# A hybrid encoder layer on one core: the first half of branch A's output projection by seven products, gate terms added by DMA, merged rows turned one block sooner

## The reference, cut to what matters

```python
proj = h @ w_in[l]                      # h: (512, 2048) after LayerNorm
...
branches = (oa * silu(ag), ob * silu(bg), oc * silu(cg))    # each (512, 1024)
merged = None
for n in range(3):
    gate = sigmoid(mg[..., n*2048:(n+1)*2048] + b_gate[l, n])
    term = gate * (branches[n] @ w_branch[l, n])            # w_branch: (3, 1024, 2048)
    merged = term if merged is None else merged + term
y = merged @ w_out[l]
h = layer_norm(alpha * h + y, ln_g[l], ln_b[l])
```

## Time and profile before

| | us |
|---|---|
| three timed runs | 1806.41, 1807.3, 1809.01 |
| their median | 1807.3 |
| profiled execution, span (no time of its own is given beside it) | 1805.6 |
| PE, DVE, ACT busy in it | 1791.1, 1368.5, 906.6 |
| stage 3 within it, four halved groups and four plain blocks | 152.4 and 92.4 |

### The profile page before, as it was taken

The page is one execution under the profiler, slowest core; times in us unless marked ns, Lnnn a source line. Parts: engine busy times, 40 slices in busy tenths (PEclk is TensorE's granted clock), DMA queues, the critical chain, the costliest instruction groups (busy, mean ns, idle before and its releaser), DMA issues.

```text
span 1805.6 us, 24177 instructions
## 1 busy us (share of the span) xinstructions
PE 1791.1 (99%) x8365; PEld 1487.6 (82%) x8365; DVE 1368.5 (76%) x2243; ACT 906.6 (50%) x1540; POOL 245.2 (14%) x313
## 2 busy tenths in 40 slices
PE   9999999999999999999999999999999999999997
PEld 7888888888888888888888888888888888888886
DVE  6777774887777877577778878788788787757778
ACT  5663332555465655444445545455555666435543
POOL 1111110100222221001000101101111000002223
PEclk9999999999999999999999999999999999999999
DMA  9576776960865545366566867868696978739989
GB/s 336 180 211 164 194 201 205 260 233 15 227 185 170 176 133 147 104 160 172 119 202 177 257 127 225 216 144 245 129 285 145 310 257 293 262 129 236 238 211 197
DMA packets 250440, 355.49 MB, mean 197 GB/s; under 512 B 14641, under 2 KB 141681, under 8 KB 247025
## 3 DMA queue, kind: packets, MB, share of 16 engines
q1 hardware_dynamic: 178640, 201.61, 35.3%
q0 software_dynamic: 71568, 152.50, 35.1%
q10 hardware_dynamic: 144, 0.26, 0.0%
HBM read 303.30 MB, written 97.11 MB: 222 GB/s over the span
## 4 chain that ended last, share of the span: by engine, by line
PE 97%; DMA 1%; DVE 1%; issue 0%; ACT 0%; POOL 0%; POOLq 0%; DVEq 0%; SPq 0%; ACTq 0%
PE acc L745 10%; PE acc L747 10%; PE acc L746 10%; PE scores L957 6%; PE scores L959 6%; PE scores L961 6%; PE acc L957 3%; PE acc L959 3%; PE acc L961 3%; PE transposed L770 3%; PE attended L959 2%; PE attended L957 2%; PE attended L961 2%; PE scores L1178 2%; PE scores L1180 2%; PE scores L1182 2%
## 5 line engine op out<-in xcount | busy, mean ns | idle before, releaser
L1428 ACT ACTIVATE piece_split<-w 128x512 fp32r<-128x512 f32 x448 | 282.8, 633 | 290.5 <-PE scores L961 104.9
L2069 DVE TENSOR_TENSOR piece_split<-w,piece_split 128x512 fp32r<-128x512 f32 x448 | 309.1, 691 | 104.0 <-ACT piece_split L1428 94.1
L1921 DVE TENSOR_TENSOR w_lo<-raw_weights,w_hi 128x1024 fp32r<-128x1024 f32 x205 | 249.2, 1220 | 140.1 <-ACT w_hi L1323 138.4
L745 PE MATMUL acc<-h_hi,w_lo 128*128 128x512 f32 x800 | 319.2, 399 | 0.0
L747 PE MATMUL acc<-h_hi,w_hi 128*128 128x512 f32 x800 | 312.5, 391 | 0.0
L746 PE MATMUL acc<-h_lo,w_hi 128*128 128x512 f32 x800 | 311.7, 390 | 0.0
L1323 ACT ACTIVATE w_hi<-raw_weights 128x1024 fp32r<-128x1024 f32 x205 | 217.0, 1060 | 130.0 <-PE acc L747 27.3
L747 PEld LDWEIGHTS acc<-h_hi,w_hi 128*128 128x128 f32 x800 | 150.2, 188 | 32.3
L745 PEld LDWEIGHTS acc<-h_hi,w_lo 128*128 128x128 f32 x800 | 150.4, 188 | 29.9 <-issue 1.8
L746 PEld LDWEIGHTS acc<-h_lo,w_hi 128*128 128x128 f32 x800 | 150.6, 188 | 28.6
L957 PE MATMUL scores<-piece_split,h_lo 128*128 128x512 f32 x384 | 149.9, 390 | 0.2 <-DVE piece_split L2069 0.2
(11 more groups left out here) (502 smaller groups left out, 3691.5 us busy)
## 6 DMA issues: line engine op xcount, KB each, us to landing
w<-in_w_in SPq DMA_DIRECT2D x128, 512.0 KB, 9.4
raw_weights<-in_w_in SPq DMA_DIRECT2D x102, 512.0 KB, 4.0
anch_weight_sums_scratch<-in_w_branch POOLq DMA_DIRECT2D x24, 1024.0 KB, 10.2
raw_weights<-in_w_branch SPq DMA_DIRECT2D x40, 512.0 KB, 5.5
raw_weights<-in_w_mem_kv SPq DMA_DIRECT2D x32, 512.0 KB, 5.6
raw_weights<-anch_weight_sums_scratch SPq DMA_DIRECT2D x32, 512.0 KB, 5.8
gate_scratch<-in_b_gate POOLq DMA_DIRECT2D x12, 1024.0 KB, 11.8
gate<-gate_scratch POOLq DMA_DIRECT2D x12, 1024.0 KB, 9.2
```

Of the source, the lines that this page charges most:

```text
L745: pe.matmul(bank_out, wl, hi[:, k, :], start=first, stop=False)
L1428: act.activation(p_split[:, n % RING, 0, :], sources[p][:, k, :], ACT.Copy).then_inc(pc_hi, 1)
L1921: dve.tensor_tensor(w_lo[:, slot, :], raw[:, slot, :], w_hi[:, slot, :].bitcast(F32), ALU.subtract).then_inc(lo_ready, 1)
L2069: dve.tensor_tensor(p_split[:, n % RING, 1, :], sources[p][:, k, :], p_split[:, n % RING, 0, :].bitcast(F32), ALU.subtract).then_inc(pc_lo, 1)
```

## The change

The constants: `HALVED` goes to 5, and two plain blocks (`PLAIN`) stay, nb = 2 and 3. The fifth halved group (s = 4) is branch A's columns 0 to 1023. Its left operands are cut from the same branch A buffer: low and high parts of four pairs of channel rows and of the sums S1 to S4, made by `branch_a_sum`, `branch_a_hi` and `branch_a_lo` in the order of the tables `A_HI` and `A_LO` at fixed steps of the fourth and fifth group. In groups s = 2, 3 and 4 three transfers a group (`add_terms`) add the gate terms to `merged_rows`; only the G4 quarter is still added by DVE. A fourth slot of weight sums, at G7, stands in each gate group. Blocks 0 and 1 are turned in chunks 1 and 2 of the first plain block, block 2 in chunk 1 of the second. The roles of PSUM banks acc and (scores 2, attended) swap behind the groups, and all counts of semaphores follow.

```diff
-CH_PLAIN = CH_M + 56
-CH_OUT = CH_PLAIN + 4 * (D // 512)
+CH_PLAIN = CH_M + 70
+CH_OUT = CH_PLAIN + 4 * (D // 512 - 2)
...
-HALVED = 4
+HALVED = 5
+PLAIN_FROM = 2
+PLAIN = D // 512 - PLAIN_FROM
...
+TERMS = 6
+MERGED_FILLS = {(0, 1): 0, (0, 2): 1, (1, 1): 2}
+A_HI = (("rows", 0), ("sum", 3), ("rows", 2), ("rows", 4), ("sum", 0), ("rows", 6), ("sum", 1), ("sum", 2))
+A_LO = (("sum", 3), ("rows", 0), ("rows", 2), ("sum", 1), ("rows", 4), ("rows", 6), ("sum", 0), ("sum", 2))
...
             def halved_product(s, p, banks, first, stop):
+                if s == HALVED - 1:
+                    pick = branch_a_tiles(p)
+                    hi, lo = pick(bra_hi, as_hi), pick(bra_lo, as_lo)
+                    needed = {G1: ("rows", 2), G5: ("sum", 3), G6: ("sum", 1), G2: ("rows", 6), G7: ("sum", 0),
+                              G3: ("sum", 2), G4: ("rows", 6)}[p]
+                    pe.wait_ge(branch_ready, 2 * PRODUCTS + A_LO.index(needed) + 1)
...
             def fill_merged(nb, j):
-                if j == 0:
-                    pe.wait_ge(m_sum, SUMMED + TT * (nb + 1))
+                if j == 0 and nb < PLAIN_FROM:
+                    pe.wait_ge(terms_added[nb], TERMS_BASE + 16 * (1 + nb) * (HALVED - 2))
+                    pe.wait_ge(m_sum, SUMMED)
+                elif j == 0:
+                    pe.wait_ge(m_sum, SUMMED + TT * (nb - PLAIN_FROM + 1))
...
-                        if m and s == 1:
-                            fill_merged(m - 1, 2 * kk)
-                            fill_merged(m - 1, 2 * kk + 1)
+                        if (m, s) in MERGED_FILLS:
+                            fill_merged(MERGED_FILLS[m, s], 2 * kk)
+                            fill_merged(MERGED_FILLS[m, s], 2 * kk + 1)
...
+            branch_a_hi_at = dict(zip(((3, 1), (3, 3), (3, 5), (3, 8), (3, 10), (3, 11), (3, 12), (4, 5)), A_HI))
...
+            branch_a_sum_at = {(3, 1): (0,), (3, 5): (1,), (3, 7): (2,), (4, 1): (3,), (4, 2): (4,)}
+            branch_a_lo_at = dict(zip(((3, 4), (3, 6), (3, 8), (4, 1), (4, 3), (4, 4), (4, 6), (4, 7)), A_LO))
...
             def halved_gates(s, b, half, src, sign):
-                if s >= 2:
-                    first = {(0, 0): 0, (1, 1): 2, (1, 0): 4}[b, half]
-                    for t in range(2):
-                        row = 2 * half + t
-                        dve.wait_ge(term_made, 6 * (s - 2) + first + t + 1)
-                        dve.tensor_tensor(sums[nb][:, row, :], sums[nb][:, row, :], gate[b][:, row, :], ALU.add)\
-                            .then_inc(m_sum, 1)
...
             def store_group(g):
-                    for n, p in enumerate((G5, G6, G2)):
+                    for n, p in enumerate((G5, G6, G2, G7)):
...
+            def add_terms(s):
+
+                for n, (b, half) in enumerate(((0, 0), (1, 1), (1, 0))):
+                    rows = slice(2 * half, 2 * half + 2)
+                    pool.wait_ge(term_made, TERMS * (s - 2) + 2 * n + 2)
+                    pool.dma_start(sums[2 * (s % 2) + b][:, rows, :], gate[b][:, rows, :], accum_op=ALU.add)\
+                        .then_inc(terms_added[b], 16)
...
-            for m in (*range(1, 2 * HALVED - 2), 2 * HALVED - 1, 2 * HALVED - 2,
-                      *range(2 * HALVED, 2 * HALVED + D // 512)):
+            for m in (1, 2, 3, 4, 5, 7, 6, 9, 8, 10, 11):
...
+                if m in (7, 9, 10):
+                    add_terms((m - 1) // 2 - 1 if m % 2 else HALVED - 1)
                 load_gate(m)
...
-                if m >= 2 * HALVED:
-                    pool.dma_start(out_t[m - 2 * HALVED], ln_b[0].partition_broadcast(P)).then_inc(preset, 16)
+                if m >= 2 * (HALVED - 1):
+                    pool.dma_start(out_t[m - 2 * (HALVED - 1)], ln_b[0].partition_broadcast(P)).then_inc(preset, 16)
```

More of the change, by code:

```diff
@@ L324, in branch_tiles, with branch_a_tiles, branch_a_part @@
         return lambda whole, summed: whole[:, rows, tok]
+    def branch_a_tiles(p):
+        if p in (G5, G6, G7, G3):
+            n = {G5: 3, G6: 1, G7: 0, G3: 2}[p]
+            return lambda whole, summed: summed[:, n, :, :]
+        return branch_tiles(p)
+    def branch_a_part(part):
+        kind, n = part
+        if kind == "sum":
+            return as_hi[:, n, :, :], as_raw[:, n, :, :], as_lo[:, n, :, :]
+        return bra_hi[:, n:n + 2, :], bra_raw[:, n:n + 2, :], bra_lo[:, n:n + 2, :]
     def branch_weights(n, half, right):
@@ L1215, in _ @@
             pe.wait_ge(ev_c12, 2 * ALL + 2)
-            for m in range(D // 512):
+            for m in range(PLAIN):
                 for s in range(4):
@@ L2615, in _ @@
                         halved_lo(1, G2 + j - 1)
-                    if s == 3 and 1 < j < 6:
-                        branch_lo(j - 2)
+                    if (s, j) in branch_a_lo_at:
+                        branch_a_lo(*branch_a_lo_at[s, j])
+                    for n in branch_a_sum_at.get((s, j), ()):
+                        branch_a_sum(n)
             def add_branch(m):
+                nb = PLAIN_FROM + m
                 dve.wait_ge(gate_ready, 2 * HALVED + m + 1)
+                dve.wait_ge(terms_added[m % 2], TERMS_BASE + 16 * (1 + m % 2) * (HALVED - 3))
                 for t in range(TT):
@@ L2631, in add_branch @@
                     dve.wait_ge(m_free, TT * m + t + 1)
[L2632 removed]
+                    dve.tensor_tensor(sums[nb][:, t, :], sums[nb][:, t, :], gate[m % 2][:, t, :], ALU.add)\
                         .then_inc(m_sum, 1)
[L2635 removed]
+            last_m = PLAIN - 1
             steps = Steps(dve, dve_once, OUT_STEPS, base=LN_STEPS + F_STEPS + PRESET_STEPS)
@@ L2672, in double_lo @@
                 dve.tensor_tensor(lo, whole, hi.bitcast(F32), ALU.subtract).then_inc(pc_lo, 1)
-            for m in range(last_m + 1):
+            for m in range(PLAIN):
                 for s in range(4):
```

142 lines of the change are left out of this document (88 added, 54 removed).

## The result

| | us |
|---|---|
| the kernel before, 20 runs | median 1807.21 (1806.16 to 1809.34) |
| the changed kernel, 20 runs | median 1810.14 (1807.58 to 1813.54) |
| ratio | 1.0015, 95% interval 1.0009 to 1.0022 |
| profiled execution of the changed kernel | 1808.13, span 1806.3 |

The change costs 2.7 us by the ratio (2.9 between the medians) instead of gaining 3.0. This is within the 0.2% (3.6 us) that I called no change, but the time is above my whole range (1801.0 to 1808.5). The profiled execution is itself 2.0 us under the median, so what follows explains the profile first and the median only in part.

The account below looks back on a forecast made before the run. PE, busy 99%, was taken to bound the kernel: span 1805.6 - 5.4 (fewer matmuls) + 2.4 (wait) = 1802.6 us. With the 1.7 us offset to the median, the forecast was 1804.3 us, range 1801.0 to 1808.5.

Parts of the forecast that it names:

- 24 matmuls at 0.2268 us, 5.4 us: Fifth halved group: 168 matmuls replace 192 of two plain column blocks, saving 5.4 us on PE.
- Gate terms: Third to fifth groups: nine 512 KB adding transfers, landing in 6.9 to 8.9 us, delay later gate loads at no cost.
- burst: Fifth group: two gate loads and two preset writes, 4 MB issued at once by POOL, slowing weight loads beside them.
- The fifth group's operands: here I expect a wait: At G7, S3's low part comes late behind chunk 9: 9.4 + 11.4 + 3.4 - 21.8 = 2.4 us of PE wait.
- slowed by each other's queue rather than by a full engine: Fifth group: loads in the burst are delayed by sharing between queues; chunk 9's landing taken as 11.4 us.
- equal halves: Fifth group: if queues' turns were equal, a load takes 9.2 us, about twice 4.6, and the wait is 0.2 us.
- Weight sums: cost 0, bounds 0 and 3: End of the first gate group: the new slot's copies finish by 997.3, or 1003.3 if consecutive; cost 0 to 3 us.
- rival 3: Extra weight sums hit the gate groups' weight loads; PE waits up to 3 us; 2 us gives 1806.3; chance 0.07.
- The earlier turning hidden by 1.3 us: Start of the plain part: first turn comes 8.2 us after the last product, its additions end at 6.9; cost 0.
- Offset of 1.7 us from span to median: Whole kernel: the earlier median, 1807.3, lies 1.7 us above the profiled span; carried over to the forecast.

Follow-up runs that it names:

- kernel 14: The changed kernel without its nine adding transfers (terms missing from the output) and with presets moved to gate loads 10 and 11: 1804.41 us, ratio 0.9984.
- kernel 1: The changed kernel without its nine adding transfers, so their gate terms are missing from the output: 1808.07 us, ratio 1.0004.
- experiment 7: The changed kernel with S3's low part made after the split of chunk 8 instead of chunk 9: 1810.58 us, ratio 1.0019.
- experiment 4: The changed kernel with one slot of weight sums moved from the first gate group that has them to the last: 1809.67 us, ratio 1.0013.
- kernel 13: On kernel 9, the low part of rows 6 and 7 made before the split of chunk 7: 1804.89 us, ratio 0.9987.
- kernel 9: The changed kernel with only the third group's gate terms added on the vector engine and presets moved to gate loads 10 and 11: 1804.85 us, ratio 0.9990.
- 2: The changed kernel with the nine adding transfers made plain copies, so the sums miss their first part: 1808.19 us, ratio 1.0005.
- 8: The changed kernel with all gate terms on the vector engine, S3's low part one step sooner, presets with gate loads 10 and 11: 1808.85 us, ratio 1.0006.
- 3: The changed kernel with the gate terms of groups 3 to 5 added on the vector engine: 1810.87 us, ratio 1.0020.
- 15: On kernel 13, three slots of weight sums in the first gate group that has them and five in the second: 1812.38 us, ratio 1.0026.

## Why the prediction was wrong

- *24 matmuls at 0.2268 us, 5.4 us.* Right: the branch stage of kernel 14 is 5.2 us shorter than before.
- *Gate terms: "Cost 0: a microsecond of ACT at most".* **This step failed.** I had the landing right (6.9 to 8.9 us taken, 5.7 to 10.4 measured) and asked only who waits for the transfer, its gate load. I did not ask what it takes from the loads beside it: weight loads took 10 to 12 us next to three of them, where the kernel before had 4 to 9. That is worth 2.0 us of the median (2.2 with the presets moved). It begins at the third group's end, one group ahead of any burst, where I had not looked, and comes out as 1.8 us at G4 of the fourth group and as the wait at G2 of the fifth.
- *"The fifth group's operands: here I expect a wait".* The mechanism is right, and kernel 1 shows its sum whole (3.0 worked out, 3.04 measured). In the changed kernel the sum is 11.7 + 9.1 + 3.4 - 21.8 = 2.4 us, and G2 and G7 together wait 2.4 (1.08 and 1.34 as distance). That this is my figure is luck: chunk 9 was issued 2.3 us later than I had, behind the additions, and landed 2.3 us sooner. The chunks behind it took 11.5, 13.5 and 12.6 us (issued from 1565.2 to 1569.7). I stopped at the first operand that was late; experiment 7 shows that removing it gives nothing. The presets alone are worth 3.4 us of the median, of which the profile's rows at G7 and G4 of the fifth group show 1.9; the rest was not found.
- *"slowed by each other's queue rather than by a full engine".* Wrong: in the kernel before the DMA share beside the same burst (1558 to 1570) is 0.96 at 360 GB/s, and in the changed kernel 0.97 at 361, so the engines were all but full. The turns, packet by packet, of the Trainium skill ("DMA: Bandwidth & Descriptors", queues, rings and completion order), read by me as equal halves, gave an estimate of 9.2 us for a load in the burst. Chunk 9's 9.1 us agrees, the 11.5 to 13.5 of the next three do not.
- *Weight sums: cost 0, bounds 0 and 3.* Mis-sized: 1.42 us in the profile, 0.4 to 1.6 in the others with four slots, in the place named by rival 3, to which I gave 0.07. The margin there was already spent (a PE wait of 0.2 and DVE's of 2.79); DVE's is now 4.05. The new slot's two copies had landed at 1001.0, within my 997 to 1003; what I left out is what they take from the weight loads beside them (12 us instead of 3.5) and from the next ones (experiment 4). It is the same omission as with the gate terms.
- *The earlier turning hidden by 1.3 us.* Right: no wait stands in the plain part.
- *Offset of 1.7 us from span to median.* 3.8 here (1810.14 against 1806.3): a run's time is 1.8 us above its span, and the profiled execution lies 2.0 under the median. The changed kernel varies more from run to run, 6.0 us from lowest to highest against 3.2. That its marginal loads are the reason is my guess and not shown. So of the 5.8 us between forecast and median, 3.7 are the waits read above, and 2.1 are this offset, with its cause open.

## What to carry to other kernels

When work is moved from an engine to a DMA, price the time that it takes from the DMA engines, and not only its landing and who waits for it: the loads next to it are the ones that pay, and they may belong to the next stage. On an engine that never waits, small waits from different places add up, and closing one uncovers the next; ask how late the whole supply is, not which operand is last. Here the remedy was to choose by place: additions on the vector engine where it has room (third group), by transfer where it has none, and nothing deferrable in a burst; kernel 13 then takes 0.9987 of the time before, 2.3 us of the 5.4. It and kernel 9 are the best of the ten complete variants, and their intervals do not allow for that choice.

## What the runs showed of the hardware

A wait of PE can cost more than its length. Behind waits of 2.04, 2.24, 3.04, 3.94 and 6.49 us (kernels 2, 8, 1, 3 and 15) the granted clock fell to its lower level (0.50 in windows laid behind each of them) and came back some 3 to 5 us after PE had started again, at 1.66, 1.67, 1.65, 2.45 and 2.56 us on top; behind the waits of up to 1.66 us of these profiles matmul spacing showed no such stretch. In all five PE had worked for over 20 us without a wait before it. So in these kernels several short waits were cheaper than one long one of the same sum.

A transfer that adds SBUF to SBUF, 512 KB, took 8.5 us to landing against 6.4 as a plain copy (medians of nine), and issuing it kept POOL for 872 ns against 534. In the stretch with three of them the DMA engines were full at 267 GB/s (share 1.04), where with the copies they carried 343 at 0.96.
